# Filler products on TensorE in front of its waits, in a two-block transformer kernel

## What is computed

```python
def hybrid_layer(x, ...):                       # first block, twice
    hn = rms_norm(x, norm_g[0])
    (nsa_q, k_c, ..., sb_v, merge_g) = split_columns(hn @ w_in)
    y_nsa = nsa_attention(...) @ w_nsa_o        # compressed + selected + window attention
    y_sb = stick_breaking_attention(...) @ w_sb_o
    gate = jax.nn.sigmoid(merge_g)
    mixed = (gate[..., :D] * y_nsa + gate[..., D:] * y_sb) @ w_out
    x = x + rms_norm(mixed, norm_g[1])
    ff = jnp.square(jax.nn.relu(rms_norm(x, norm_g[2]) @ w_ff1)) @ w_ff2
    return x + rms_norm(ff, norm_g[3])

# second block: x (512 tokens) and ctx (256 tokens), modulated by silu(c) @ ada_w
# layer 0: latent attention (MLA) over 768 tokens, then a squared-ReLU MLP
# layer 1: gated linear attention (GLA), then a squared-ReLU MLP, 512 tokens
    h = modulate(rms_norm_2(x, norm_g[i, 0]), m[:, 0], m[:, 1])
    x = x + m[:, 2] * rms_norm_2(mixer(h), norm_g[i, 1])
    h = modulate(rms_norm_2(x, norm_g[i, 2]), m[:, 3], m[:, 4])
    x = x + m[:, 5] * rms_norm_2(sqrelu_mlp(h, w1, w2), norm_g[i, 3])
```

## Time and profile before

| | us |
|---|---|
| median of 3 runs | 3885.91 |
| lowest, highest | 3882.39, 3888.79 |
| the profiled execution, its own time | 3886.2 |
| its span, first to last instruction | 3884.4 |

### The profile page before, as it was taken

One profiled execution on the slowest core, in us unless ns is written; L12 is line 12 of the kernel. 1 busy time (PEld: TensorE's weight loads), 2 busy tenths in 40 slices (PEclk: granted clock), 3 DMA queues, 4 the chain that ended last, 5 costly groups with the idle time before them and its releaser, 6 DMA issues. The chain is left out here.

```text
span 3884.4 us, 45612 instructions
## 1 busy us (share of the span) xinstructions
PE 3497.9 (90%) x17364; PEld 2838.9 (73%) x17364; DVE 1920.2 (49%) x2408; ACT 1355.8 (35%) x1980; POOL 552.6 (14%) x389
## 2 busy tenths in 40 slices
PE   7887989999788798999977988999999688889998
PEld 5665868887566586888756877788887577757886
DVE  4373337777337333777735651533332544455443
ACT  3265234443326523444323442321222333323222
POOL 0141003334014100333300110000000100010000
PEclk9988999999898898999988999999999899989998
DMA  3101223442210122344210001111111011102221
GB/s 131 68 1 46 96 108 141 162 151 76 88 68 1 51 94 105 141 158 155 76 49 17 23 28 55 44 65 65 61 58 44 33 44 44 44 32 87 97 89 62
DMA packets 58340, 287.09 MB, mean 74 GB/s; under 512 B 9824, under 2 KB 11104, under 8 KB 30944
## 3 DMA queue, kind: packets, MB, share of 16 engines
q1 hardware_dynamic: 58208, 285.34, 20.8%
HBM read 283.21 MB, written 2.10 MB: 73 GB/s over the span
## 5 line engine op out<-in xcount | busy, mean ns | idle before, releaser
L163 PE MATMUL ps<-h_hi,w_hi_rest 128*128 128x512 f32 (+1 forms) x1072 | 390.3, 364 | 38.7 <-DVE w_lo_rest L152 22.5
L164 PE MATMUL ps<-h_lo,w_hi_rest 128*128 128x512 f32 (+1 forms) x1072 | 369.9, 360 | 0.0
L1246 POOL TENSOR_TENSOR ada_context<-ada_context,ada_scaled 128x768 f32<-128x768 f32 x112 | 287.6, 2568 | 462.0 <-ACT ada_scaled L1331 456.9
L152 DVE TENSOR_TENSOR w_lo_mix<-w_raw,w_hi_mix 128x2048 fp32r<-128x2048 f32 x96 | 221.6, 2310 | 262.0 <-ACT w_hi_mix L146 261.9
L166 PE MATMUL ps<-h_hi,w_lo_rest 128*128 128x512 f32 (+1 forms) x1072 | 327.2, 360 | 0.0
L163 PE MATMUL ps<-h_hi,w_hi_mix 128*128 128x512 f32 x768 | 303.5, 395 | 17.3 <-DVE w_lo_mix L152 12.7
L164 PE MATMUL ps<-h_lo,w_hi_mix 128*128 128x512 f32 x768 | 302.4, 394 | 0.0
L166 PE MATMUL ps<-h_hi,w_lo_mix 128*128 128x512 f32 x768 | 302.3, 394 | 0.0
L350 POOL TENSOR_TENSOR x<-x,y 128x512 f32<-128x512 f32 (+1 forms) x32 | 63.8, 1994 | 1597.3 <-DVE y L356 1597.3
L255 PE MATMUL ps<-sq,consts 128*128 128x512 f32 (+1 forms) x372 | 178.0, 627 | 120.6 <-ACT sq L230 120.6
L146 ACT ACTIVATE w_hi_rest<-w_raw 128x2048 fp32r<-128x2048 f32 x82 | 156.3, 1908 | 359.9 <-PE ps L166 357.0
(11 more groups left out here) (385 smaller groups left out, 7798.9 us busy)
## 6 DMA issues: line engine op xcount, KB each, us to landing
w_raw<-in_stream SPq DMA_DIRECT2D x205, 1024.0 KB, 4.8
ada_raw<-in_ada_w SPq DMA_DIRECT2D x128, 384.0 KB, 5.2
cmp_w<-in_cmp_w SPq DMA_DIRECT2D x8, 1024.0 KB, 7.4
mla_raw<-in_stream SPq DMA_DIRECT2D x8, 512.0 KB, 3.5
x<-in_x SPq DMA_DIRECT2D x1, 2048.0 KB, 9.1
out<-x SPq DMA_DIRECT2D x1, 2048.0 KB, 7.3
x<-in_ctx SPq DMA_DIRECT2D x1, 1024.0 KB, 11.4
consts<-in_consts SPq DMA_DIRECT2D x1, 832.0 KB, 11.8
```

The source lines that it names most:

```text
L152: dve.tensor_tensor(k.wlo[:, n % 2, 0:width], k.raw[:, n % 2, 0:width], k.whi[:, n % 2, 0:width].bitcast(F32), ALU.subtract).then_inc(k.w_ ...
L163: pe.matmul(out, whi, xhi, start=start, stop=False)
L164: pe.matmul(out, whi, xlo, start=False, stop=False)
L1246: pool.tensor_tensor(ada.context, ada.context, ada.scaled[:, j % 2, :], ALU.add).then_inc(m["context"], 1)
```

## The change

`keep_busy` issues `count` products of `ones` by the identity (128x128, f32) into 128 columns of a PSUM bank that nobody reads. They carry no semaphore. They are put at these places of TensorE's list:

- in a norm: 5 before the sums of `pe_all` (9 for the norm of `x` in `stage_mlp`), 4 before the wait for the root, 2 before the wait for the diagonal tiles; into bank 3. A norm in bank 6 (that of the GLA heads) has none (`pause` is false);
- in `first_tiles`: 5 at 512 tokens, 8 at 768, before the wait for the first `h_lo`; into bank 4;
- at the start of merge 13, of the projection `wo` 8, of `mla_o` 14, of values 18; into bank 4.

```diff
--- before.py
+++ after.py
@@ -199,6 +199,12 @@
 
 
 
+def keep_busy(pe, k, count, bank=4):
+
+    for _ in range(count):
+        pe.matmul(k.ps[:, bank * 512:bank * 512 + P], k.c["ones"], k.c["ident"], start=True, stop=True)
+
+
 class Norm:
 
 
@@ -213,6 +219,7 @@
     def __init__(self, k, name, src, kt, tok, bank, it=0, sems=None):
         self.k, self.src, self.kt, self.tok, self.bank, self.it = k, src, kt, tok, bank, it
         self.nt = tok // P
+        self.free, self.pause = 3, bank != 6
         self.name = name
         self.sems = sems or [k.sem(f"{name}_{s}") for s in self.NAMES]
         self.squared, self.summed, self.root, self.column, self.inverse, self.diag, self.spread = self.sems
@@ -256,17 +263,20 @@
                              start=t == 0, stop=t == self.kt - 1)
         last.then_inc(self.summed, 1)
 
-    def pe_all(self, pe):
+    def pe_all(self, pe, before=5):
+        keep_busy(pe, self.k, before * self.pause, self.free)
         for t in range(self.kt):
             self.pe_add(pe, t)
         self.pe_spread(pe)
 
     def pe_spread(self, pe):
+        keep_busy(pe, self.k, 4 * self.pause, self.free)
         pe.wait_ge(self.root, 1 + self.it)
         for j in range(self.nt):
             last = pe.matmul(self.stat[:, j:j + 1], self.k.root[:, j * P:(j + 1) * P], self.k.c["ones"][0:1, 0:1],
                              start=True, stop=True)
         last.then_inc(self.column, 1)
+        keep_busy(pe, self.k, 2 * self.pause, self.free)
         for j in range(self.nt):
             pe.wait_ge(self.diag, j + 1 + self.nt * self.it)
             last = pe.matmul(self.rb[:, j * P:(j + 1) * P], self.k.c["ones"], self.k.diag[:, j * P:(j + 1) * P],
@@ -380,6 +390,7 @@
 
     outs = [tile_out(k, j, tok)[1] for j in range(count)]
     w = [unit_tiles(k, n, 0, KT, cols, j) for j in range(count)]
+    keep_busy(pe, k, 3 * (tok // 256) - 1)
     for i in range(KT):
         x_wait(i)
         xs = [(k.hhi[:, i, c0:c0 + cw], k.hlo[:, i, c0:c0 + cw]) for c0, cw in chunks(tok)]
@@ -1036,6 +1047,7 @@
 
         @block.tensor
         def _(pe):
+            keep_busy(pe, k, 13)
             with pe.Fori(0, TURNS) as it:
                 for pr in range(PAIRS):
 
@@ -1133,7 +1145,7 @@
     return n0 + UNITS_MERGE
 
 
-def stage_project(nc, k, name, stream, n0, xhi, xlo, y, tok, last_unit, y_norm=None, split=0):
+def stage_project(nc, k, name, stream, n0, xhi, xlo, y, tok, last_unit, y_norm=None, split=0, pause=8):
 
 
 
@@ -1147,6 +1159,7 @@
 
         @block.tensor
         def _(pe):
+            keep_busy(pe, k, pause)
             for j in range(KT):
                 if j % 2 == 0:
                     unit_ready(pe, k, n0 + j // 2)
@@ -1251,7 +1264,7 @@
                 n_post.pe_all(pe)
             else:
                 n_post.pe_spread(pe)
-            n_pre.pe_all(pe)
+            n_pre.pe_all(pe, 9)
             unit_ready(pe, k, n0)
             first_tiles(pe, k, n0, 256, 2, tok, lambda i: normed.pe_wait(pe, i), s["ready"])
 
@@ -1648,6 +1661,7 @@
 
         @block.tensor
         def _(pe):
+            keep_busy(pe, k, 18)
             unit_ready(pe, k, n0)
             for j, (t, g) in enumerate(outs):
                 if j >= ring:
@@ -2342,7 +2356,7 @@
         n = stage_key_rope_values(nc, k, b, down[:, 5, :], stream, n)
         n = stage_latent_attention(nc, k, b, stream, n)
         rings(k, "rest", 175)
-        n = stage_project(nc, k, "mla_o", stream, n, k.hhi, k.hlo, y, TOK, UNITS_2)
+        n = stage_project(nc, k, "mla_o", stream, n, k.hhi, k.hlo, y, TOK, UNITS_2, pause=14)
     with k.sem_scope():
         n = stage_mlp(nc, k, "mlp0", stream, n, y, hid_hi, hid_lo, TOK, parts_of(b, 0, 1, TOK), parts_of(b, 0, 2, TOK, 3), UNITS_2)
         stage_residual(nc, k, "mlp0r", y, TOK, parts_of(b, 0, 3, TOK))
```

## The result

| | before | after |
|---|---|---|
| median, us | 3887.35 | 3860.24 |
| lowest, highest | 3882.39, 3889.50 | 3859.04, 3863.95 |
| the profiled execution, its own time | 3886.2 | 3859.0 |
| its mean granted clock | 0.942 | 0.960 |

The medians are of four runs each. The changed kernel takes 0.9934 of the time before (95% interval 0.9916 to 0.9951), 27.1 us less. A second series of five runs gave 3860.72 (3857.70 to 3863.08), 0.9933 [0.9920, 0.9947].

A forecast was written before the change was run, and what follows sets the result against it. TensorE alone was taken to bound the large stages, its clock at 0.50 around idle seams. Gains (a) to (e) of 36.5 us less losses (f) to (i) of 10.3 made net 26.2 off 3886.2: 3860 us, range 3848 to 3877.

The forecast's parts named there:

- (a): First dense tiles of a stage, seven sites: fillers give back half of the time at 0.50; gain 14.5 us.
- (b): Diagonal products at 0.50 in nine norms: 0.2 to 0.9 us each, 1.3 in one 768-wide norm; gain 6.6 us.
- (c): Sums of squares in the norms: dips at 0.50 partly given back; gain 5.7 us.
- (d): Merge: thirteen fillers in its idle time give back 2.8 and 2.2 us in the two layers; gain 5.0 us.
- (e): MLA output projection and values: busy time at 0.50 gives back 2.3 and 2.4 us; gain 4.7 us.
- (g): Values and mla_o: fillers begun at the low clock overhang the free time by 1.7 and 1.4 us; loss 3.1 us.
- (f): Output projection wo: eight fillers delay its ready products by 1.8 us, twice, and the dip stays; loss 3.7 us.
- (h): Norms down, ckv, mlp0, gate1 begin with the clock down: 0.6 us lost each; loss 2.4 us (bounds -2 and 4.8).
- (i): Four fillers before root waits: 0.15 us in each of five block-opening norms, 0.3 before the last MLP's norm; loss 1.1 us.
- The first: Slower: fillers don't hold the clock up, all 36.5 us of gains go, losses total 18; 3904 us, chance 0.06.
- Half-kept: Clock still falls at half of the sites, gain 8 to 9 us, or at a third, 14; about 3873, chance 0.22.
- The third: Nothing measurable: (g) and (h) at upper bounds (+6) on top of half-kept gains; 3883 us, chance 0.08.

The follow-up runs named there:

- e1: Changed kernel with every filler's moving operand cut from 128 columns to one; 3908.84 us, 1.0054 of the kernel before.
- e4: Changed kernel without the fillers in first_tiles (5 or 8 behind the diagonal products), all others kept; 3872.59 us.
- e9: The changed kernel once more, unedited, as the mark for the second series; 3860.72 us (3857.70 to 3863.08, five runs).
- e2: Changed kernel without the eight fillers in front of the projection wo; 3855.67 us, 3.4 below the profiled execution of the changed kernel.
- e11: Same kernel as e2, timed in rounds in the second series; 3855.88 us, 4.8 below the changed kernel's median there.
- e6: Changed kernel with the fillers for wo, cq, ckv, mlp0 and gate1 moved to the tail of the stage before, values 17 for 18; 3842.66 us.
- e3: Changed kernel without the five fillers ahead of the sums in down, ckv, mlp0's first norm and gate1; 3860.85 us once.
- e10: Same kernel as e3, timed in rounds; 3861.59 us (3858.51 to 3863.92), where the changed kernel had 3860.72.
- e8: Changed kernel plus fillers in GLA norms, the moves of e6, fillers at rope's tail, and 3 for 4 before block-opening root waits; 3829.40 us, 0.9856 of before.

## Why the prediction was right, and where its terms were off

The total was 3860.0 and came out at 3860.2. Part of that is luck: several terms missed by 1 to 2 us, 2.7 came from places that the sum leaves out, and they cancelled. By the ledger of the one profiled pair:

| term | forecast | ledger |
|---|---|---|
| (a) first tiles: seven sites forecast, eight found | +14.5 | +14.0 |
| (b) diagonal products | +6.6 | +8.8 |
| (c) sums | +5.7 | +5.6 |
| (d) merge | +5.0 | +4.5 |
| (e) less (g), values and `mla_o` | +1.6 | +1.4 |
| (f) `wo` | −3.7 | −3.6 |
| (h) norms that begin low | −2.4 | −4.1 |
| (i) root waits | −1.1 | −2.2 |
| places not in the sum | 0 | +2.7 |

- **The mechanism** held, and two runs show it: the first tiles, merge and the sums of (c) are at 1.00 after, and e1, the same count of fillers with one column, lost all of the gain and more. Products by `ones` with an identity as moving operand, which the trace of before did not have, hold the upper level here: the mean is 1.00 over 30 us (560 to 590) in after. The halves in (a), (d) and (e), from work that takes twice its time at 0.50, stand too: in before dense products of `wo` start 0.43 us apart in the dip (506.53, 506.96), and 1653 of the feed-forward took 353.96 us at 1.00, 0.21 each; a filler's record takes 0.21 and 0.11.
- **(a)** The two qkv stages gave 1.3 and 2.2 (forecast 1.4 and 1.7), the feed-forwards 2.3 and 2.5 (2.6 and 2.8), the last MLP 2.2. The missing part is in `down` (0.8) and `mlp0` (1.4), for which I had about 2 each. Against it stands an eighth site that the forecast left out: `gate1` has first tiles and their fillers too, and won 1.3. Its spread was at 1.00 before already (twelve records in 1.60 us); it is the first product behind 3.66 us of idle time that was low. Before, then after:
```profile
3049.23 0.76 PE L163 MATMUL ps<-h_hi,w_hi_rest 128*128 128x512 f32 x1 [3.66 <-DVE h_lo L311]
```
```profile
3027.66 0.49 PE L163 MATMUL ps<-h_hi,w_hi_rest 128*128 128x512 f32 x1 [1.78 <-DVE h_lo L321]
```
  e4 shows a second error under a right sum: the feed-forwards' first tiles were kept up by the fillers in the norm before, not by the five in front of them.
- **(b)** was mis-sized, low by a quarter: nine norms gave 7.5 together, and `ckv` 1.3, as forecast. I had spread 0.2 to 0.9 over the sites; six of the nine gave 0.88 to 0.92, the whole difference between a spread at 0.50 and one at 1.00, such as 2.07 and 1.16 us. The second layer's qkv is one of the six, by luck: e9 has its spread at 2.07 still, as the prediction said of this norm. The site of the earlier trace rows in after:
```profile
1536.27 1.16 PE L282 MATMUL ps<-diag,consts 128*128 128x128 f32 x8
```
- **(f)** is the term that was best founded, and the rows after say it in the forecast's own words: first real product later, dip still there. e2 and e11 put it at 3.4 and 4.8 us for the two sites, and e6 shows the other half of it: 14 fillers one stage earlier in place of the 8 turn a loss of 1.8 a site into a gain of 1.6. That the dip has a fixed length, as the prediction has it, holds for before, after and e2 (3.4 us each), not for e1 (6.8).
- **(g)** In values the 36 records took 5.88 us, not 7.7, since the clock was still up as they began and down for 3.4 us of them only (2054.3 to 2057.7); both net sums came out near the forecast, +0.9 for values and +0.5 for `mla_o` (0.7 and 0.9).
- **(h)** The sign I took is not shown. The ledger has 4.1 lost, but e3 and e10, which take these fillers away, are no faster: 3861.6 for 3860.7. The delay of the sums is real, about 2 us over the four, and so is what the fillers give back, in part in stages behind the norm. The bounds of −2 to 4.8 held this; the value of 2.4 was half a guess.
- **(i)** was twice the forecast: in five block-opening norms 0.35 each, not 0.15. The eight records take 1.05 us, and the wait they stand in front of was 0.77 long; the difference of 0.3 is paid in full. That is why e8 takes 3 products there; it was not tried alone.
- **Places not in the sum** add 2.7: +0.5 in the first norm, +1.9 as the second layer's qkv opens, +0.8 as the second block does, +0.7 in compression, −1.5 and +1.2 in the attentions, −0.9 in the GLA. No run tested them as such. In stick-breaking they change sign from turn to turn (−1.4, +1.1, +0.3, −1.5), which would fit dips that fall on other work; and e9 against after has steps of the same size there with no edit at all (+0.9, −0.7, +1.5 in the first layer).
- **The rivals.** The first (3904) was realised by e1 at 3909: its price was about right in total, if not term by term, and its condition was false. Half-kept (3873) would have needed dips left at half of the sites; after has none in first tiles or merge, but in `wo`, as forecast, and where the norms of (h) open, which was low before too. The third has a slip in its sum: (g) and (h) at their upper bounds (5.1 and 4.8) are 4.4 us above what the forecast took (3.1 and 2.4), not 6.
- **Readings.** Every digit of the clock's row is a 9 or an 8, not every second one; a 9 stands for full speed too, and only the eleven 8s say that it was not held. The stretch of 522 us that the prediction calls the first sub-block of the second model is the 768-token MLP. Neither changes the sum.

## What to carry to other kernels

Where TensorE is the bound and its granted clock falls behind each seam, as here, products that nobody reads are worth a try. Those 128 columns wide took 27.1 us off this kernel, those of one column made it 0.5% slower than before (e1). They won where they lay in time that was idle anyway: in front of a wait that is longer than they are, or at the tail of the stage before (e6, 16.4 us more). At the head of `wo`, in front of operands that were ready, they cost their full time (1.8 us a site), and the dip came all the same, 0.8 us behind the start of the first of them. Count them by the price at the level at which they will run, 0.11 or 0.21 us a record here, and look at the tail of the stage before first: fillers there and in the norms that had none won more (31 us) than the whole change (27 us). Try each place by itself: in the norms that begin low they brought nothing.

## What the runs showed of the hardware

- An f32 product with one column cost TensorE as much here as one with 128 columns: 0.11 us a record at 1.00 for either (eight in 0.95 us in e1, in 1.05 in after, the last one's tail in it). At 0.50 36 one-column records took 7.81 us in e1, 0.21 to 0.22 a record, and ten of 128 columns 2.47 us in e9, 0.21: twice as much for either.
- TensorE's busy time did not tell its clock: from 560 to 590 e1 had it busy in 28.34 of 30 us at a mean of 0.72, after in 27.08 at 1.00.
- The same idle time of 2.32 us was followed by a product at the upper level (0.47 us) in one place of e4 and by one at the lower (0.77 us) in another, where the spread ahead of it was at the lower one already (2.08 us against 1.16).
- Of the time still idle in e8 the three largest pieces stand in front of the first fillers behind a change of section: 24.0 us at the entry of the second block, 21.0 between the two layers of the first, and 17.3 at the start of the program. In the first two VectorE and GpSimd finish the residual in some 9 us, and for most of the rest no engine computes; no run touched them. TensorE's waits in e8:
```profile
PE ps L205 <- PEq L1535: 24.0, 1, 24.0
PE ps L205 <- issue: 21.0, 1, 21.0
PE ps L205 <- PEq L1478: 17.3, 1, 17.3
```
